# Eight gathered V rows of the first block taken in attention, and table u's stage left with 40

## The reference, cut to what matters

```
def block(args):
    xb, ib, gb = args
    a = jax.nn.gelu(jnp.einsum('ted,td->te', u[ib], xb), approximate=False)
    return jnp.einsum('te,ted->td', gb * a, v[ib])
```

## Time and profile before

| what | value |
|---|---|
| device time, median of 3 runs | 4274.88 us (4254.72 to 4291.08) |
| span of the profiled execution, first to last instruction | 4071.2 us |
| median less span | 203.7 us |
| PE busy / DVE busy / ACT busy / POOL busy | 95% / 75% / 35% / 39% |
| mean granted TensorE clock | 0.977 |
| DMA | 1310.11 MB, mean 322 GB/s |

### The profile page before, as it was taken

One profiled execution on the slowest core, in us unless ns is written; L12 is line 12 of the kernel. 1 busy time (PEld: TensorE's weight loads), 2 busy tenths in 40 slices (PEclk: granted clock), 3 DMA queues, 4 the chain that ended last, 5 costly groups with the idle time before them and its releaser, 6 DMA issues. The chain is left out here.

```text
span 4071.2 us, 69892 instructions
## 1 busy us (share of the span) xinstructions
PE 3866.5 (95%) x26178; PEld 3688.7 (91%) x26178; DVE 3055.7 (75%) x4082; ACT 1421.4 (35%) x2046; POOL 1588.5 (39%) x1350
## 2 busy tenths in 40 slices
PE   7999999999999897999899999999996999999997
PEld 7999988999999665988799999998996999999997
DVE  5875167777777433878679999999975888888887
ACT  5785122222222223223333333333332333333332
POOL 0000022332222111225245766776464555555551
PEclk9999999999999998999899999999997999999998
DMA  6988879999999896888678888988997999999996
GB/s 235 346 310 298 289 278 341 346 360 367 357 358 364 294 385 246 309 330 337 260 278 291 327 322 315 341 308 289 375 341 272 355 345 343 346 343 346 342 331 252
DMA packets 336018, 1310.11 MB, mean 322 GB/s; under 512 B 48880, under 2 KB 105360, under 8 KB 266272
## 3 DMA queue, kind: packets, MB, share of 16 engines
q1 hardware_dynamic: 201648, 646.09, 43.5%
q0 software_dynamic: 108848, 629.71, 42.0%
q10 hardware_dynamic: 25344, 31.99, 2.1%
HBM read 1237.86 MB, written 69.77 MB: 321 GB/s over the span
## 5 line engine op out<-in xcount | busy, mean ns | idle before, releaser
L2369 POOL DMA_INDIRECT routes_scratch<-gate_sums,route x384 | 461.8, 1203 | 117.0 <-issue 117.0
L129 PE MATMUL acc<-x_hi,w_hi 128*128 128x448 f32 x1296 | 476.7, 368 | 9.9 <-DVE x_lo L1363 6.7
L129 PE MATMUL acc<-x_lo,w_hi 128*128 128x448 f32 x1296 | 474.8, 366 | 0.0
L129 PE MATMUL acc<-x_hi,w_lo 128*128 128x448 f32 x1296 | 474.8, 366 | 0.0
L113 ACT ACTIVATE w_hi<-w_raw 128x1024 fp32r<-128x1024 f32 x242 | 256.0, 1060 | 618.7 <-DMA w_raw<-in_w_gate 253.1
L118 DVE TENSOR_TENSOR w_lo<-w_raw,w_hi 128x1024 fp32r<-128x1024 f32 x242 | 295.6, 1223 | 212.5 <-ACT w_hi L113 211.2
L2770 POOL TENSOR_TENSOR tile_full<-act_and_gate 128x320 f32<-128x320 f32 x120 | 318.1, 2651 | 260.2 <-DVE tile_lo L2869 178.3
L2191 PE MATMUL acc<-h_hi,w_hi_a 128*128 128x320 f32 (+1 forms) x1152 | 371.0, 322 | 21.4 <-DVE w_lo_a L2181 20.4
L2173 ACT ACTIVATE w_hi_a<-w_raw 128x1024 fp32r<-128x1024 f32 x272 | 281.3, 1057 | 299.8 <-PE acc L2934 253.1
L2191 PE MATMUL acc<-h_hi,w_hi_b 128*128 128x320 f32 (+1 forms) x1152 | 367.1, 319 | 19.7 <-DVE w_lo_b L2181 19.2
L2173 ACT ACTIVATE w_hi_b<-w_raw 128x1024 fp32r<-128x1024 f32 x272 | 279.3, 1055 | 260.1 <-PE acc L2934 211.3
(11 more groups left out here) (510 smaller groups left out, 10380.2 us busy)
## 6 DMA issues: line engine op xcount, KB each, us to landing
w_raw<-in_w_peer_u SPq DMA_DIRECT2D x256, 512.0 KB, 6.7
w_raw<-in_w_peer_v SPq DMA_DIRECT2D x256, 512.0 KB, 5.9
w_first<-in_w_gate SPq DMA_DIRECT2D x96, 512.0 KB, 5.0
w_raw<-in_w_gate SPq DMA_DIRECT2D x96, 512.0 KB, 7.1
w_first<-in_w_z SPq DMA_DIRECT2D x66, 512.0 KB, 5.3
w_raw<-in_w_z SPq DMA_DIRECT2D x66, 512.0 KB, 7.6
k_ring<-in_cache_k SPq DMA_DIRECT2D x64, 512.0 KB, 6.3
v_ring<-in_cache_v POOLq DMA_DIRECT2D x64, 512.0 KB, 7.9
```

The lines of the kernel that those rows point to most:

```text
L129: last = nc.tensor.matmul(dst, l_, r_[:, cc, 0:cn], start=(cc == first and p_ == 0), stop=(cc == last_c and p_ == 2))
L2369: pool.indirect_dma_start(route_dram, bass.IndirectOffsetOnAxis(ap=route[0:ROWS[b], b, n:n + 1], axis=0), gsum[0:ROWS[b], h % SUMS, b - 1, ...
```

## The change

Eight V jobs (`JOBS_A` = 8, rows 152 to 159 of the list) move to attention; the merge's jobs follow them in the list, and table u's stage keeps 40 instead of 48. Row 0 of the eight is gathered in the preparation stage, into `ring_first0`, and summed at the end of DVE's step 1. Row 1 goes into the same slot, from POOL's queue ahead of value page 8, and is summed at the end of step 6. Rows 2 to 7 are gathered after POOL's last value load into three slots on top of `k_ring`, once all key loads have been used; they are summed at the end of steps 34, 35, 36, 37, 38 and 38. Row 5 waits for row 2's slot, row 6 for row 3's, row 7 for row 4's. `qzm` (query rows for cross-attention) moves to another place, since row 0 lies on its old one.

```
-        JOBS_Z, JOBS_M, JOBS_O = 152, 20, 36
+        JOBS_Z, JOBS_A, JOBS_M, JOBS_O = 152, 8, 20, 36
...
+        A_LATE = 2
+        ring_a = [ring_f[0], *(at(f"ring_late{k}", [P, D], F32, O_K + k * D * 4) for k in range(3))]
+        def slot_a(r):
+            return 0 if r < A_LATE else 1 + (r - A_LATE) % 3
+        def gather_late(pool, r):
+            e = JOBS_Z - NEXP + r
+            pool.indirect_dma_start(ring_a[slot_a(r)][:], None, a["peer_v"], bass.IndirectOffsetOnAxis(ap=eidx_first[:, e:e + 1], axis=0)).then_inc(s_arow[slot_a(r)], 16)
...
                 nc.gpsimd.memset(ones[:], 1.0).then_inc(s_ones, 1)
+                gather_late(pool, 0)
...
+        A_STEPS = [1, 6, 34, 35, 36, 37, 38, 38]
+        A_PAGE = 8
...
+                        if j == A_PAGE:
+                            pool.wait_ge(s_aused, 1)
+                            gather_late(pool, 1)
                         if j >= RING_V:
                             pool.wait_ge(s_vu, j - RING_V + 1)
                         pool.dma_start(v_ring[:, j % RING_V, :], source(item, "v", pool)).then_inc(s_vl[j % RING_V], 16)
+                pool.wait_ge(s_ku, len(page_no))
+                for r in range(A_LATE, JOBS_A):
+                    if r >= A_LATE + 3:
+                        pool.wait_ge(s_aused, r - 2)
+                    gather_late(pool, r)
...
+                    for r in range(JOBS_A):
+                        if A_STEPS[r] == p:
+                            k = slot_a(r)
+                            take_v_row(dve, JOBS_Z + r, s_arow[k], (s_aused, r), 16 * ((r - A_LATE) // 3 + 1 if r >= A_LATE else r + 1), ring_a[k][:])
...
-        JOBS_U = NEXP * 2 - JOBS_Z - JOBS_M - JOBS_O
+        JOBS_U = NEXP * 2 - JOBS_Z - JOBS_A - JOBS_M - JOBS_O
```

More of the change, by code:

```diff
@@ L1429, in build @@
         s_cc = sem("c_parts")
+        s_arow = [sem(f"attention_row_gathered{k}") for k in range(4)]
+        A_LATE = 2
[5 more added lines that the diff above has]
+            pool.indirect_dma_start(ring_a[slot_a(r)][:], None, a["peer_v"], bass.IndirectOffsetOnAxis(ap=eidx_first[:, e:e + 1], axis=0)).then_inc(s_arow[slot_a(r)], 16)
         def first_pages(eng):
@@ L1480, in _ @@
                     last.then_inc(s_vtp, 1)
-        recycle(keep=s_kl)
+        recycle(keep=[*s_kl, *s_arow])
         v_ring = at("v_ring", [P, RING_V, 1024], F32, O_Z + V0 * TB * 4)
@@ L1497, in build @@
         o_s = at("sample_result", [P, 512], F32, O_V)
-        qzm = at("qzm", [P, 4, MEM * 40], F32, O_R1T)
+        qzm = then("qzm", [P, 4, MEM * 40], F32)
         assert place[0] <= O_W + 32768 and O_V + 2048 <= O_ZT
@@ L1554, in build @@
         s_ku, s_vu = sem("k_page_used"), sem("v_page_used")
+        s_aused = sem("attention_row_used")
+        A_STEPS = [1, 6, 34, 35, 36, 37, 38, 38]
+        A_PAGE = 8
         s_qz, s_qc = sem("q_rows_placed"), sem("q_rows_cleared")
@@ L1932, in v_job @@
         def v_job(pool, m):
-            gather_first(pool, JOBS_Z + m, s_row, s_rused, m % 3, m - 2)
+            gather_first(pool, JOBS_Z + JOBS_A + m, s_row, s_rused, m % 3, m - 2)
         def v_row(dve, m):
-            take_v_row(dve, JOBS_Z + m, s_row[m % 3], (s_rused, m), 16 * (m // 3 + 1), ring_f[m % 3][:])
+            take_v_row(dve, JOBS_Z + JOBS_A + m, s_row[m % 3], (s_rused, m), 16 * (m // 3 + 1), ring_f[m % 3][:])
         O_T = O_X1 + NB * D * 4
@@ L2383, in gather @@
                         pool.wait_ge(s_head, n // PTOP + 1)
-                    e = JOBS_Z + JOBS_M + JOBS_O - NEXP + n
+                    e = JOBS_Z + JOBS_A + JOBS_M + JOBS_O - NEXP + n
                     table, at_ = ("peer_u", eidx[:, 0, n:n + 1]) if kind == "u" else ("peer_v", eidx_first[:, e:e + 1])
```

## The result

The changed kernel takes 4299.97 us (median of 18 runs), the kernel before beside it 4276.85; ratio 1.0045, 95% interval 1.0029 to 1.0062: 19 us longer, where 6 us shorter was forecast and the range ended at 4291.

What follows compares the result with a forecast made beforehand. Transfers were taken to bound most of attention, POOL's late gathers the end of table u's stage. Terms -20.1 - 2 + 2 + 4 + 10 = -6 us gave span 4065, time 4269 us, range 4250 to 4291.

Steps and rivals of the forecast that it cites:

- Row 1: Attention, step 6: DVE holds until the row lands, PE comes 7 us late, part won back; +4 us, bounds 2.6 and 7.
- L: Row 1's landing time after its gather's issue at 1419.4; taken as 10 us, making PE L - 3.0, 7 us late.
- PE's transposes of step 8, on which all of PE's queue waits: Attention: unit 7's maximum, queued behind DVE's hold, delays PE from step 8, at 1425.51, by about 7 us.
- what cannot be won back is the MB itself: Attention, row 1: loads continue during the hold and PE catches up, except for the transfer's 2.6 us.
- The first rival: Attention, DVE's hold in step 6 without recovery: slower from L = 11.5, 4281 to 4289 us at L 17 to 25; chance 0.18.
- the 203.7 us: Difference between profiled span 4071.2 and the timed median, taken to lie around the span and left unchanged.
- my -22: Table u's stage: -20.1 us for stripes 137 to 143 and -2 for stripes 120 to 127.
- Row 0: Preparation stage and step 1: its 1.05 MB go ahead of first key pages; +2 us, bounds 0 and +2.6.
- The tail: End of attention, rows 2 to 7: DVE ends later, uncovered before the merge's barrier; +10 us, bounds +8 and +11.2.
- The last stripes: Table u's stage, stripes 137 to 143: POOL's gathers serve rows needed later, so all three stalls go; -20.1 us.
- the second and fourth rivals: Table u's stage: POOL still binds its end, net +6, chance 0.1; or weights or DVE bind, net +16, chance 0.05.
- the smallest slack is about 7 us: Table u's stage: after the change each late gathered row lands at least about 7 us before its stripe needs it.

Runs made afterwards that it cites:

- the faster condition: Jobs where the kernel before takes near 4070 us; there the changed kernel, unedited, beside the kernel before measured 1.0010, +4 us.
- the slower condition: Jobs where the kernel before takes near 4260 us; there the changed kernel against the kernel before measured 1.0045 and, run again unedited, 1.0055.
- the first job: The changed kernel's first timing beside the kernel before: 4299.97 us against 4276.85, ratio 1.0045.
- the second repeat of the kernel before: The kernel before run again without edit for another trace: span 4063.7, time 4065.41 us.

## Why the prediction was wrong

**Row 1 is the step that failed in both conditions.** I priced it at +4 with bounds 2.6 to 7; it costs 15.1. Three things were wrong in that step. L was 13.7, not 10 (12.1 to 13.7 in the four traces with a row in step 6). "PE's transposes of step 8, on which all of PE's queue waits": PE was held one step earlier, by the drain of unit 4, which I had left out of what is queued behind DVE's wait. And "what cannot be won back is the MB itself" was wrong twice: PE came out of the hold at 1.2 GHz, for 12 us in this trace, and the transfers, which are the stage's limit, stood still with their slots full until PE, at half its clock, had worked its way to the next page. The first rival had the hold without recovery, at a chance of 0.18: with L = 13.7 its formula gives 2.6 + 10.7 + 11 - 22, +2; the faster condition measured +4. It did not have the earlier step, the clock or the stopped transfers, so that its sum comes this close is in part luck.

**The base was the second.** I took the 203.7 us between span and median for time around the span. They were the distance between the two conditions. All rows came from one in which stage u is some 175 us shorter than in the timed runs, and my -22 was made for it.

**Row 0:** +2 forecast. The fourth drain into `b_t` comes 60.2 us after the projection in the eight traces with row 0, 58.3 in the twelve without: +1.9. Single traces lie from 54.0 to 62.9, so that it meets the +2 so well is luck.

**The tail:** +10 forecast, 10.8 measured (28.5 against 17.7). The steps were as written, row 7's wait for a lone gather included.

**The last stripes:** -20.1 forecast, 60.4 to 62.3 became 42.2; 116 to 137 gave 3.4 instead of 2 (151.5 to 148.1). Right in the faster condition, and there the second and fourth rivals are out. One reading was off without harm: "the smallest slack is about 7 us" leaves out the last row, which by the same sum had 6.5 less 4.5, 2 us. In the changed kernel of the faster condition it is gathered at 3092.94 and summed 11.8 us later, without a wait. In the slower one the last six gain 15.6, but 116 to 137 take 11 to 13 more than in the one trace of before. From 116 on it is 211.4 us before, 206.7 and 208.6 after: about -4. +26.3 and -4 make +22, where +19 and +23 were measured; that sum takes the stage up to stripe 116 as unchanged, which the traces are too far apart to show.

**What stays open.** The 11 to 13 us in the slower condition. In the first job's trace of the changed kernel the two slips of these stripes, of 7 us each, lie between 3221 and 3275, and the waits there are

```profile
DVE w_lo_b L2210 <- issue: 9.4, 1, 9.4
...
PE acc L2220 <- issue: 6.7, 9, 1.4
```

so it is these gaps again and no row. But the kernels with five rows in attention have 156.7 and 171.7 in these stripes, and the sums from stripe 116 to the end go from 195 (two scatters, all 48 rows) to 212 (43 rows) over the seven traces of this condition: it scatters, and one trace of before is thin. So that the gain of stage u shrinks in the slower condition rests on few traces; that the change costs more there, +19 and +23 against +4, rests on the timed runs. Up to stripe 116 the traces of the slower condition differ by 50 us among themselves (1048 to 1099), with no order by kernel. What makes the condition was not tried.

The part that attention wins back is small: 1.9 + 15.1 + 10.8 is 27.8, and attention grew by 26.3.

## What to carry to other kernels

Before a wait goes onto an engine, list everything that engine does between it and the next idle moment, drains of a shared bank first, and find the earliest of another engine's steps that needs one of them. In a stage limited by transfers, a stop costs nothing only while ring slots are left to fill; ask also how much work stands between the end of the stop and the next slot that is freed. When the end of a stage is bound by one queue, reordering it moves the bound to whatever the next stage reads from it: compare the queue's last instruction with the barrier, too. And when a span and the timed runs differ by more than their spread, get a trace from the condition that is timed before pricing anything.

## What the runs showed of the hardware

One program has two levels of time: medians of 4069.85 to 4073.53 us in three jobs (on two chips, one of them twice), 4251.54 to 4276.85 in three others (two on further chips, the first without a record of its chip). No job had both, so it may go by chip; no chip was seen at both levels, and only one was met twice. Of the 188 us between two traces of the kernel before (spans 4064.2 and 4252.5), 175 lie between the first and the last drain of table u's stage, in stretches in which PE, ACT and DVE all have gaps on "issue". Over all kernels that stage takes 1074 to 1103 us on the one kind and 1255 to 1305 on the other. Why was not tried.

PE's granted clock fell to 0.50 as the hold of 11.8 us began and stayed there for 12 us of work after it; in three more traces with holds of 12.2 to 13.2 us it rose 6 to 12 us after PE went on. Attention of the unchanged computation differs by 11 us between traces (250.1 to 261.1), most of it before the fourth drain into `b_t` (54.0 to 61.7 us after the projection). In the second repeat of the kernel before (span 4063.7) the granted clock was 0.50 from 1396.5 to 1410.2, where the first trace has 1.00; which of the two is cause and which effect was not tried.

A gather of 1 MB took 7.5 us from issue to use when alone (1625.41 to 1632.95) and 13.7 in a full queue (1421.14 to 1434.87). By the fit of the Trainium skill (DMA: Bandwidth & Descriptors, "Anatomy of one DMA") it would be an estimated 4.4 us; the trace disagrees and decides.
